# Taking the sixteen best scores straight from PSUM, beside the query projections

## The chip, the cores and the metric

The kernel runs on one core of a Trainium2 chip. The metric is the device time of one launch in microseconds (us). One launch computes one layer of the network over 1,024 tokens, all in fp32.

## The reference

The layer is an attention and state-space mixer followed by PEER, a feed-forward block that looks up single-neuron experts, and by a gated embedding. The change concerns only the look-up. Cut to that part, the reference is:

```python
q  = (u @ w_query).reshape(b, s, 8, 2, 128)            # 8 heads, 2 sides
sc = einsum("bshtd,htkd->bshtk", q, sub_keys)           # 128 scores a side
top_s, top_i = top_k(sc, 16)                            # sixteen best of each side
cand_s = top_s[..., 0, :, None] + top_s[..., 1, None, :]   # 256 sums
best_s, best_pos = top_k(cand_s, 16)
best_i = cand_i at best_pos                             # cand_i = top_i[0] * 128 + top_i[1]
gates  = softmax(best_s)
act    = gelu(einsum("td,ted->te", x, expert_u[best_i])) * gates
out    = einsum("te,ted->td", act, expert_v[best_i])
```

So each token picks 8 x 16 = 128 experts, and each of them needs one row of `expert_u` and one of `expert_v`, 4 KB each.

## The kernel before, in words

The tokens are cut into 8 tiles of 128 (one token per partition), and the tiles into 4 groups of 2. All five engines walk through one list of steps, `whole_program`, in the same order, and each does its own part of a step. A semaphore counts what others have finished.

**Ahead of the slots.** `before_slots` (L240) lists what must be done before the first expert is fetched: the whole front (mixer) of group 0, its query unit 0, the score selection for the first two (tile, head) pairs, and query unit 1, which stands ahead of these selections.

**The slots.** A slot n (`slot_steps`, L193) stands for one expert of every token of a tile: 128 slots a tile, 16 slots a head, 1,024 in all and 44 more at the end. In a slot POOL issues the indirect DMA (512 KB) that gathers 128 rows of `peer_u` (L868, a ring of 6) and, 44 slots later, 128 rows of `peer_v` (L880, a ring of 8). POOL takes both in turn. DVE multiplies a `peer_u` row with the normalised token and sums it (`dot`, L1575), and PE adds up the weighted `peer_v` rows (L2017). A gather of `peer_u` waits until DVE has done the dot product six slots earlier.

**Work beside the slots.** `beside_slots` (L248) hangs other steps on slots: query units 2 and 3 of group 0 on slots 2 to 20; the fronts of groups 1, 2 and 3 with their four query units on slots 22 to 204, 204 to 456 and 456 to 708 (`FRONT_SPANS`), where each step is placed by its share of the sum of the costs in `PACE`; and the gate of each tile later. Weight blocks of 1 MB come through a ring of 4 (L637); SP issues them in list order.

**A query unit** (`query_steps`, L169) is four head sides for two tiles: the projection (`p`, PE L1754, copied by ACT L956), the transposition (`q_t`, PE L1968, ACT L1121), and the score product (`q_s`, PE L1976), which fills one PSUM bank with 4 x 128 scores per token. ACT copies the bank to SBUF (L1128), SP writes it to HBM (`keep_scores`, L728, 256 KB), and later reads it back head by head (`scores_in`, L734, 128 KB). There are 32 such (tile, unit) pairs and 64 (tile, head) pairs kk.

**The selection** (`top`, L1519) for head kk goes over DVE in six steps, on slots 2, 4, 6, 8, 10 and 12 of the sixteen of an earlier head: steps 0 and 1 take the sixteen best of each side with `sixteen_best` (L1512: MAX8, FIND_INDEX8, MATCH_REPLACE8, MAX8, FIND_INDEX8), step 2 forms the 256 sums, step 3 takes the sixteen best of these, steps 4 and 5 work out the expert numbers. The read-back for the next head is issued on slot 8 (`s_in`).

PSUM banks are shared: `plan_banks` (L322) gives each step the bank that has lain unused longest, out of four once slot 25 is reached, and PE waits until the bank's last content has been taken.

## Time and profile before

| | |
|---|---|
| time before, median of 3 runs | 3769.55 us (3768.69 to 3770.98) |
| the profiled execution, its own time | 3753.05 us |
| its span in the trace | 3751.3 us |
| DVE busy | 2232.2 us (60%) |
| PE busy | 2475.1 us (66%) |
| POOL busy | 1964.5 us (52%) |
| moved by DMA | 1320.09 MB, mean 352 GB/s |

The page's header and its section 2 cut the span into 40 slices of 94 us: "DMA" is the mean busy share of the 16 DMA engines, in tenths. The windows give the same for chosen stretches. Their columns are: stretch and length; busy us of PE, of PE's weight loads, of DVE, ACT and POOL, each with its number of instructions in brackets; TensorE's granted clock; DMA share; GB/s. A window of one line has only the busy time of that line, and then the last three. DVE runs two instructions for a dot product at L1575, so half of that number is the slots passed. "Idle before" in a group of instructions is the time its engine stood still just ahead of them, and the arrow names what ended it. In a timeline the number in square brackets is that idle time for one instruction. A DMA share of slightly over 1 comes about because packets of two queues overlap on one DMA engine.

### The profile page before, as it was taken

The page shows a single profiled execution, that of the slowest core. Times are in us where ns is not written, and L with a number is a line of the kernel's source. Part 1 is how long each engine was busy: PE and PEld are TensorE (multiplying, and loading weights), DVE is VectorE, ACT ScalarE, POOL GpSimd, SP SyncE. Part 2 cuts the span into 40 slices and gives each one's busy share as a digit, 9 for nine tenths or more (in the row PEclk, how much of TensorE's full clock was granted, in tenths as well). Part 3 has the DMA queues.
Part 4 walks back from the last instruction along what each step waited for, and adds up shares of the span by engine and source line. Part 5 has one row for each costly group of instructions (what it writes and reads, how often), then busy time and mean ns, then how long its engine had stood idle before and what let it go on. Part 6 is the DMA issues. An engine that isn't in the chain of part 4 may idle for free. (4 is left out here: it accounts for less than half of the span.)

```text
span 3751.3 us, 33795 instructions
## 1 busy us (share of the span) xinstructions
PE 2475.1 (66%) x10840; PEld 1198.8 (32%) x10840; DVE 2232.2 (60%) x5446; ACT 765.6 (20%) x1750; POOL 1964.5 (52%) x2064
## 2 busy tenths in 40 slices
PE   8869688777777758666777767677725534443554
PEld 5644345443333434322333434322301101110111
DVE  2330868566556766675556766776556666666640
ACT  2331222231112222321122222311111111011010
POOL 0000455545555656555555656655656666666663
PEclk9879899778888777778888877778867666766778
DMA  7325899989999999999999999999999999999995
GB/s 229 114 74 188 317 398 385 352 315 355 406 405 404 376 346 390 384 350 406 405 405 403 369 364 384 382 377 407 401 376 381 372 387 382 378 385 377 367 377 202
DMA packets 427462, 1320.09 MB, mean 352 GB/s; under 512 B 54280, under 2 KB 75920, under 8 KB 425112
## 3 DMA queue, kind: packets, MB, share of 16 engines
q0 software_dynamic: 294912, 1073.87, 74.1%
q1 hardware_dynamic: 132376, 244.06, 17.9%
q8 instruction: 89, 1.46, 0.2%
q14 instruction: 85, 0.70, 0.0%
HBM read 1290.69 MB, written 32.60 MB: 353 GB/s over the span
## 5 line engine op out<-in xcount | busy, mean ns | idle before, releaser
L1575 DVE CUSTOM_DVE_ANT_0 u_ring<-u_ring,ps 128x1024 f32<-128x1024 f32 x1024 | 1231.7, 1217 | 551.4 <-DMA u_ring<-peer_u,idx_u 454.5
L868 POOL DMA_INDIRECT u_ring<-peer_u,idx_u x1024 | 981.5, 958 | 960.6 <-DVE idx_u L1553 379.8
L880 POOL DMA_INDIRECT v_ring<-peer_v,idx_v x1024 | 978.4, 955 | 787.1 <-PE ps L2017 340.4
L2017 PE MATMUL ps<-v_ring,spread 128*32 128x512 f32 x4096 | 752.7, 864 | 851.3 <-DMA v_ring<-peer_v,idx_v 744.2
L2017 PEld LDWEIGHTS ps<-v_ring,spread 128*32 128x32 f32 x4096 | 150.8, 138 | 1233.1 <-issue 1231.0
L1754 PE MATMUL ps<-front 128*128 128x512 f32 x1024 | 458.5, 604 | 2.1 <-ACT front L1117 2.1
L1754 PEld LDWEIGHTS ps<-front 128*128 128x128 f32 x1024 | 194.7, 194 | 271.5 <-issue 271.1
L1950 PE MATMUL ps<-front 128*128 128x512 f32 x512 | 232.8, 613 | 13.6 <-DVE front L1491 8.4
L1873 PE MATMUL ps<-front 128*128 128x256 f32 x768 | 197.8, 415 | 1.4 <-issue 1.4
L1873 PEld LDWEIGHTS ps<-front 128*128 128x128 f32 x768 | 156.1, 209 | 58.1 <-issue 34.6
L1950 PEld LDWEIGHTS ps<-front 128*128 128x128 f32 x512 | 98.9, 197 | 151.6 <-issue 151.6
L1382 DVE CUSTOM_DVE_ANT_0 front<-ps,front 128x640 f32<-128x640 f32 (+2 forms) x64 | 42.1, 658 | 154.2 <-PE ps L1841 59.0
L2047 PE MATMUL ps<-front 128*128 128x512 f32 x256 | 123.7, 637 | 13.9 <-issue 10.6
L1404 DVE SCALAR_TENSOR_TENSOR front<-front,taps 128x256 f32<-128x256 f32 x144 | 69.8, 485 | 100.0 <-ACT hist L1026 59.4
L1938 PE MATMUL ps<-front 128*128 128x512 f32 x256 | 120.8, 627 | 1.9 <-issue 1.9
L1841 PE MATMUL ps<-front 64*128 64x128 f32 x480 | 83.9, 328 | 31.9 <-DVE front L1375 9.8
L1851 PE MATMUL ps<-ident,front 128*128 128x128 f32 x240 | 49.0, 334 | 78.5 <-ACT front L1010 68.9
L1865 PE MATMUL ps<-front 128*128 128x64 f32 x480 | 76.7, 305 | 19.0 <-issue 18.6
L1841 PEld LDWEIGHTS ps<-front 64*128 64x128 f32 x480 | 72.1, 228 | 51.4 <-issue 40.0
L1149 ACT ACTIVATE dots<-dots 128x32 f32<-128x32 f32 x32 | 7.3, 229 | 396.9 <-DVE dots L1575 282.9
L1575 DVE DVE_READ_ACCUMULATOR2_ANT dots<- 128x1 f32 x1024 | 84.5, 83 | 0.0
L1865 PEld LDWEIGHTS ps<-front 128*128 128x128 f32 x480 | 70.2, 220 | 39.3 <-issue 36.4
(232 smaller groups left out, 2725.9 us busy)
## 6 DMA issues: line engine op xcount, KB each, us to landing
front<-w_in SPq DMA_DIRECT2D x76, 1024.0 KB
front<-w_out SPq DMA_DIRECT2D x32, 1024.0 KB
front<-peer_w_query SPq DMA_DIRECT2D x32, 1024.0 KB
u_ring<-peer_u,idx_u POOLq DMA_INDIRECT x1024
v_ring<-peer_v,idx_v POOLq DMA_INDIRECT x1024
front<-c_bias_all SPq DMA_DIRECT2D x32, 320.0 KB
front<-x SPq DMA_DIRECT2D x16, 512.0 KB
front<-cs_rows SPq DMA_DIRECT2D x8, 1024.0 KB
```

The source lines that it names most:

```text
L868: nc.gpsimd.indirect_dma_start(k.u_ring[:, n % RU, :], None, io["peer_u"][0], bass.IndirectOffsetOnAxis(ap=k.idx_u[:, t % 2, j:j + 1], axi ...
L880: nc.gpsimd.indirect_dma_start(row, None, io["peer_v"][0], bass.IndirectOffsetOnAxis(ap=k.idx_v[:, m % 2, column:column + 1], axis=0)).the ...
L1404: ins = stt(a, k.raw[:, c % 2, j:j + NG], k.taps[:, c, j:j + 1], a, ALU.mult, ALU.add)
L1575: nc.vector.tensor_tensor_reduce(out=row, in0=row, in1=k.un_ps, scale=1.0, scalar=0.0, op0=ALU.mult, op1=ALU.add, accum_out=k.dots[:, t % ...
L1754: last = mm(ps, k.uT[:, half * WCH + c, cols(t)], w[:, c, :], start=(half == 0 and c == 0), stop=(half == 1 and c == WCH - 1))
L1841: last = mm(ps[:, n * P:(n + 1) * P], k.qT_c[side, i // 2, cols(t)], k.kT_c[side, i // 2, kt % 6, :], start=True, stop=True)
L1865: last = mm(ps[:, at:at + HD], k.pT[:, no % 2, j, :], k.v_c[:, kt % 6, i * HD:(i + 1) * HD], start=(kt == c_keys(t)[0]), stop=(kt == t))
L1873: last = mm(ps[:, 0:NG], w[j // WCH][:, j % WCH, c % 4 * P:(c % 4 + 1) * P], k.uT[:, j, :], start=(j == 0), stop=(j == DCH - 1))
L1938: last = mm(ps, k.uT[:, c, cols(t)], w[c // WCH][:, c % WCH, :], start=(c == 0), stop=(c == DCH - 1))
L1950: last = mm(ps, k.yT[:, k.o_chunks[part] + j, cols(t)], w[:, j, :], start=(part == 0 and j == 0), stop=(part == 3 and j == WCH - 1))
L2017: last = mm(k.acc_ps[32 * j:32 * j + 32, half * 512:(half + 1) * 512], centres[:, at:at + 32], row[:, half * 512:(half + 1) * 512], start= ...
L2047: last = mm(ps[:, half * 512:(half + 1) * 512], k.fT[:, c, :], k.wg[:, c, half * 512:(half + 1) * 512], start=(c == 0), stop=(c == DCH - 1))
```

## The change

The sixteen best of each side are taken by DVE directly from the PSUM bank, in new steps `q_top` (one for each side of a unit, four for each tile and unit, 128 in all). Their values and key numbers (converted to float) lie in `best_out` and go to HBM, 64 KB a (tile, unit) pair; they are read back two heads at a time. ACT's copy of the scores goes. `top` keeps four steps, on slots 2, 4, 6 and 8. `spread_tops` puts two `q_top` steps behind each of the following steps of the query unit. `PACE` counts each `q_top` as 1.6, so the query units take a larger part of each front's slots. Query unit 1 of group 0 now stands behind the selections of the first two heads.

```diff
-        out += [(st, t, u) for st in ("q_t", "q_s") for t in tiles_of(g)]
+        out += [(st, t, u) for t in tiles_of(g) for st in ("q_t", "q_s")]
+    return spread_tops(out)
+
+def spread_tops(steps):
+    out, late = [], []
+    for step in steps + [None, None]:
+        if step:
+            out.append(step)
+        now, late = late[:2], late[2:]
+        out += now
+        if step and step[0] == "q_s":
+            late += [("q_top", *step[1:], i) for i in range(4)]
...
-            n2_t=1.2, q_t=1.2, q_s=1.2)
+            n2_t=1.2, q_t=1.2, q_s=1.2, q_top=1.6)
...
-    if 2 <= k < TILES * PH and 2 <= s <= 12 and s % 2 == 0:
+    if 2 <= k < TILES * PH and 2 <= s <= 8 and s % 2 == 0:
         out.append(("top", k, s // 2 - 1))
...
-    if k + 1 < TILES * PH and s == 8:
-        out.append(("s_in", k + 1))
+    if k % 2 and k + 1 < TILES * PH and s == 10:
+        out.append(("s_in", (k + 1) // 2))
...
-    out = front_steps(0) + query_steps(0, [0]) + [("un_in", 0), ("s_in", 0), ("s_in", 1), ("un", 0)] + query_steps(0, [1])
+    out = front_steps(0) + query_steps(0, [0]) + [("un_in", 0), ("s_in", 0), ("un", 0)]
     for k in range(2):
-        out += [("top", k, i) for i in range(6)] + [("g_exp", k), ("g_norm", k)]
-    return out + [("s_in", 2)]
+        out += [("top", k, i) for i in range(4)] + [("g_exp", k), ("g_norm", k)]
+    return out + query_steps(0, [1]) + [("s_in", 1)]
...
     def keep_scores(t, u):
-        copied(("q_s", t, u))
         n = score_no(t, u)
+        sp.wait_ge(k.best_kept, 4 * (n + 1))
...
-    def scores_in(kk):
-        n = score_no(kk // PH, kk % PH // 2)
+    def scores_in(pair):
+        n = score_no(pair // QUERY_UNITS, pair % QUERY_UNITS)
         sp.wait_ge(k.sc_out[n % 2], (n // 2 + 1) * 16)
-        if kk >= 2:
-            sp.wait_ge(k.idx_full, kk - 1)
+        if pair >= 2:
+            sp.wait_ge(k.idx_full, 2 * (pair - 1))
...
-    def q_s(t, u):
-        _, ps, copied_ = filled(("q_s", t, u))
-        o = t // GT * QUERY_UNITS + u
-        if o:
-            act.wait_ge(k.sc_out[t % GT], o * 16)
-        act_fn(k.sc[:, t % GT, :], ps, ACT.Copy).then_inc(copied_, 1)
...
+    def q_top(t, u, i):
+        _, ps, copied_ = filled(("q_s", t, u))
+        o, place = t // GT * QUERY_UNITS + u, t % GT
+        if o and i == 0:
+            dve.wait_ge(k.sc_out[place], o * 16)
+        src, vals = ps[:, i * PK:(i + 1) * PK], k.best_out[:, place, 0, i, :]
+        chain.link(nc.vector.max(vals[:, 0:8], src))
+        chain.link(nc.vector.max_index(k.keys_out[:, 0:8], vals[:, 0:8], src))
+        nc.vector.match_replace(k.beaten, vals[:, 0:8], src, -3e38).then_inc(copied_, 1)
+        dve.wait_ge(copied_, k.bank["q_s", t, u].begin + i + 1)
+        chain.link(nc.vector.max(vals[:, 8:16], k.beaten))
+        chain.link(nc.vector.max_index(k.keys_out[:, 8:16], vals[:, 8:16], k.beaten))
+        nc.vector.tensor_copy(k.best_out[:, place, 1, i, :], k.keys_out).then_inc(k.best_kept, 1)
+        n = t // GT * GT * QUERY_UNITS + u * GT + place
+        dve.wait_ge(k.best_kept, 4 * n + i + 1)
```

In `top` the two `sixteen_best` calls over 128 scores and the conversion of the key numbers are gone; the sums, the sixteen best of them and the arithmetic of expert numbers stay, and read `s_in` instead of `top` and `top_f`.

## Rows read from the trace of the kernel before

**Rows 1.** The page: busy tenths of the DMA engines in 40 slices.

```profile
DMA  7325899989999999999999999999999999999995
```

**Rows 2.** Windows by stage: ahead of the slots, slots 0 to 48, fronts of groups 1 to 3, the rest.

```profile
0.00:385.00 385.00, 317.40 (x1136) 197.06 (x1137) 105.29 (x276) 114.33 (x273) 4.67 (x16) 0.88 0.46 150
...
400.00:498.00 98.00, 54.53 (x197) 31.34 (x200) 89.85 (x222) 22.05 (x44) 52.01 (x54) 0.81 0.95 351
498.00:1070.00 572.00, 451.01 (x2026) 237.81 (x2019) 364.15 (x906) 148.62 (x347) 301.12 (x314) 0.85 0.97 370
1070.00:1905.00 835.00, 590.74 (x2733) 292.72 (x2732) 539.53 (x1324) 184.52 (x425) 483.23 (x504) 0.81 0.99 385
1905.00:2720.00 815.00, 577.75 (x2668) 289.83 (x2666) 539.89 (x1324) 180.91 (x420) 480.37 (x502) 0.81 1.00 387
2720.00:3640.00 920.00, 413.30 (x1786) 124.72 (x1786) 574.44 (x1344) 101.38 (x216) 597.97 (x628) 0.68 0.98 379
```

**Rows 3.** The waits in total, longest first, and DVE's for a row of values.

```profile
DVE u_ring L1575 <- DMA u_ring<-peer_u,idx_u: 454.5, 277, 6.0
...
DVE idx_v L1567 <- remote: 55.6, 12, 13.4
```

**Rows 4.** Timeline of DVE, the selection for head 0 ahead of the slots (side 0 of two).

```profile
375.29 0.30 DVE L1513 MAX8 top<-s_in 128x8 f32<-128x128 f32 x1 [26.30 <-DMA s_in<-scores]
...
377.14 0.30 DVE L1513 MAX8 top<-s_in 128x8 f32<-128x128 f32 x1
...
378.98 0.18 DVE L1526 CAST top_f<-top_i 128x32 f32<-128x32 uint32 x1
379.20 0.42 DVE L1527 TENSOR_TENSOR cand<-top 128x256 f32<-128x256 f32 x1
```

**Rows 5.** Timeline of ACT, SP, DVE and POOL, from the first scores to the first dot product.

```profile
368.69 0.60 ACT L1128 ACTIVATE front<-ps 128x512 f32<-128x512 f32 x1 [0.39 <-PE ps L1976]
...
369.31 1.26 SPq L731 DMA_DIRECT2D scores<-front  x2
...
372.17 0.81 SPq L739 DMA_DIRECT2D s_in<-scores  x2
...
385.65 1.09 POOL L868 DMA_INDIRECT u_ring<-peer_u,idx_u  x1 [379.82 <-DVE idx_u L1553]
...
399.68 1.19 ACT L956 ACTIVATE front<-ps 128x512 f32<-128x512 f32 x2
400.15 1.22 DVE L1575 CUSTOM_DVE_ANT_0 u_ring<-u_ring,ps 128x1024 f32<-128x1024 f32 x1
...
402.85 0.60 ACT L1128 ACTIVATE front<-ps 128x512 f32<-128x512 f32 x1 [0.63 <-PE ps L1976]
```

**Rows 6.** Groups by shape on DVE: the same operation with a source in PSUM and in SBUF.

```profile
L1471 DVE TENSOR_TENSOR front<-ps,front 128x512 f32<-128x512 f32 x16 | 11.0, 687 | 5.9 <-PE ps L1925 3.7 <-remote 2.2
...
L1464 DVE TENSOR_TENSOR front<-front 128x512 f32<-128x512 f32 x16 | 11.0, 685 | 0.0
```

**Rows 7.** The page: DMA queues and their share of 16 engines.

```profile
q0 software_dynamic: 294912, 1073.87, 74.1%
q1 hardware_dynamic: 132376, 244.06, 17.9%
```

**Rows 8.** The DMA issues by tensor: KB of one.

```profile
scores<-front SPq DMA_DIRECT2D x32, 256.0 KB
s_in<-scores SPq DMA_DIRECT2D x64, 128.0 KB
```

**Rows 9.** Windows: slots 178 to 204, the query stage of group 1.

```profile
973.00:1067.00 94.00, 78.51 (x310) 35.27 (x309) 49.73 (x126) 18.18 (x37) 52.78 (x56) 0.93 1.03 406
```

**Rows 10.** Windows of L1575 alone: slots 0 to 44, and the stretch above.

```profile
400.00:492.00 92.00, 52.37 (x89) 0.81 0.95 347
...
973.00:1067.00 94.00, 31.57 (x53) 0.93 1.03 406
```

**Rows 11.** DMA queue of SP: what its issue waited for, the wait that goes.

```profile
SPq L738 <- DVE idx_u L1553: 203.3, 8, 51.1
```

More of the change, by code:

```diff
@@ L325, in plan_banks @@
     singles = dict(n1_t=1, sub=1, a_k=GT, a_turn=1, c_turn=1, a_t=1, c_u=1, x=3, z=1, dt=1, cs=5, b_turn=2, b_cb=2, b_off=1, b_diag=1,
-                   b_state=1, y_t=1, n2_t=1, q_t=1, q_s=1, rows=1, w_turn=1, g_p=1, g_t=1)
+                   b_state=1, y_t=1, n2_t=1, q_t=1, q_s=4, rows=1, w_turn=1, g_p=1, g_t=1)
     early = before_slots()
@@ L453, in __init__ @@
         self.q = in_yT(0, 1024).rearrange("p (b n) -> p b n", n=UNIT)
-        self.sc = in_yT(1024, 1024).rearrange("p (b n) -> p b n", n=UNIT)
+        self.best_out = in_yT(1024, 256).rearrange("p (b k s n) -> p b k s n", b=GT, k=2, n=TOPK)
+        self.keys_out = self.front.bitcast(U32)[:, 10240 + 1280:10240 + 1280 + TOPK]
+        self.beaten = in_yT(1280 + TOPK, PK)
         self.xn = arena(6144, 2048).rearrange("p (t n) -> p t n", n=D)
@@ L503, in __init__ @@
         self.wT = sb("wT", [P, PART])
[L504 to L507 removed]
+        self.s_in = sb("s_in", [P, 2, 2, 4, TOPK])
         self.cand = sb("cand", [P, TOPK, TOPK])
@@ L530, in __init__ @@
         self.after = dram("after", (SEQ, D))
-        self.scores = dram("scores", (TILES * PH, P, 2 * PK))
+        self.scores = dram("scores", (TILES * QUERY_UNITS, P, 8 * TOPK))
         self.cs_rows = dram("cs_rows", (TILES * B_HEADS, P))
@@ L815, in sync_program @@
             keep_tiles(*at)
-        elif kind == "q_s":
-            keep_scores(*at)
+        elif kind == "q_top" and at[2] == 3:
+            keep_scores(*at[:2])
         elif kind == "s_in":
@@ L1242, in scalar_program @@
             q_t(*at)
-        elif kind == "q_s":
-            q_s(*at)
         elif kind == "g_exp":
@@ L1517, in sixteen_best @@
         chain.link(nc.vector.max_index(idx[:, 8:16], vals[:, 8:16], scratch))
-    def top(kk, step):
-        if step < 2:
-            if step == 0:
-                dve.wait_ge(k.sc_here[kk % 2], (kk // 2 + 1) * 16)
-            part = k.s_in[:, kk % 2, step * PK:(step + 1) * PK]
-            sixteen_best(k.top[:, step, :], k.top_i[:, step, :], part, part)
-        elif step == 2:
-            chain.link(nc.vector.tensor_copy(k.top_f[:], k.top_i[:]))
-            chain.link(tt(k.cand[:], k.top[:, 0, :].unsqueeze(2).broadcast_to([P, TOPK, TOPK]),
-                          k.top[:, 1:2, :].broadcast_to([P, TOPK, TOPK]), ALU.add))
-        elif step == 3:
+    def q_top(t, u, i):
[13 more added lines that the diff above has]
+        dve.wait_ge(k.best_kept, 4 * n + i + 1)
+    def top(kk, step):
+        kept = k.s_in[:, kk // 2 % 2]
+        sides = slice(kk % 2 * 2, kk % 2 * 2 + 2)
+        if step == 0:
+            if kk % 2 == 0:
+                dve.wait_ge(k.sc_here[kk // 2 % 2], (kk // 4 + 1) * 16)
+            first, second = kept[:, 0, kk % 2 * 2, :], kept[:, 0, kk % 2 * 2 + 1, :]
+            chain.link(tt(k.cand[:], first.unsqueeze(2).broadcast_to([P, TOPK, TOPK]),
+                          second.unsqueeze(1).broadcast_to([P, TOPK, TOPK]), ALU.add))
+        elif step == 1:
             if kk:
@@ L1533, in top @@
             sixteen_best(k.best[:], k.best_i[:], flat, flat)
-        elif step == 4:
+        elif step == 2:
             if kk == 0:
@@ L1542, in top @@
             by_side = k.hot[:].rearrange("p (a s) b -> p a s b", a=2)
-            chain.link(tt(by_side, by_side, k.top_f[:].unsqueeze(2).broadcast_to([P, 2, TOPK, TOPK]), ALU.mult))
+            chain.link(tt(by_side, by_side, kept[:, 1, sides, :].unsqueeze(2).broadcast_to([P, 2, TOPK, TOPK]), ALU.mult))
             chain.link(nc.vector.tensor_reduce(k.halves[:], by_side, axis=AX.X, op=ALU.add))
@@ L1662, in vector_program @@
             n2(*at)
+        elif kind == "q_top":
+            q_top(*at)
         elif kind == "top":
```

14 lines of the change are left out of this document (5 added, 9 removed).

## The prediction

> **What bounds the kernel now.** I read the busy shares of the 40 slices first, then windows by stage, the waits, and last the timeline around the first gather. The slices show DMA at 9 tenths or full in nearly every slice from the sixth on, and at 2 to 7 before [rows 1]. The windows put it in numbers. Ahead of the first gather (0 to 385 us) the share is 0.46: PE's front sets the time there. From 498 to 3640 us it is 0.97, 0.99, 1.00 and 0.98, while DVE is at 60 to 67% and POOL at 50 to 65% [rows 2]. DVE's longest wait is for a gathered `peer_u` row, 454.5 us in all [rows 3]. So from slot 48 on the DMA engines are the limit, and an engine counts only where it makes them run dry. Full they read 1.03 and 406 GB/s, as in a query stage [rows 9]; measured against 1.03, the four stages lose 33, 32, 24 and 45 us, 134 us together. Between 400 and 498 us both are near their limit: DVE 89.85 of 98 us busy, DMA 0.95 [rows 2]. Here DVE sets the pace of the slots, because `peer_v` is not yet gathered. Two currencies follow: a microsecond of DVE on the way to slot 44 is paid in full, one taken out later is paid only in as far as DMA ran dry for it; a byte saved is worth its DMA time after slot 44.
>
> **Price of one new step.** `sixteen_best` over 128 scores runs from 375.29 to 377.14, 1.85 us; the conversion of the indices with its gap takes 0.22 us [rows 4]. `q_top` is the same chain with a conversion of its own: 2.07 us. Its source is now PSUM. No MAX8 on PSUM is in the trace; an addition of 128x512 takes 687 ns with a source in PSUM and 685 ns from SBUF [rows 6], so I take no surcharge (bounds: 0, and 5% of the 1.85 us, some 3 us over all that lie ahead of slot 44). 128 steps cost 265 us of DVE, against the 64 x 3.9 = 250 us that go (375.29 to 379.20, two sides and the conversion): DVE's sum is nearly unchanged, its place is not. ACT loses 32 copies of 0.60 us [rows 5], which nobody waited long for: 0.
>
> **A. To the first gather and the first dot product.** Before, ACT's copy starts at 368.69, the write is issued at 369.31, the read at 372.17, DVE begins at 375.29, and POOL gathers at 385.65 [rows 4, 5]. After, DVE takes four sides of tile 0 first: 368.7 + 4 x 2.07 = 377.0. Its write can go, but SP stands in list order before the write of tile 1, whose four sides DVE ends at 385.3; only then can it issue the read. With 1.1 us of issuing and the 3.1 us from issue to data (372.17 to 375.29) DVE has the sixteens at 389.5. What is left of the selection took 379.20 to 385.65, 6.4 us: first gather at 395.9, **+10.2 us**. The first dot product stood at 400.15, 14.5 us after the first gather; 3.9 us of that are side selections that go: 406.5. But now query unit 1 stands between. PE's projection of it needs nobody and has 40 us for it, but ACT copies it only after `g_exp(1)`, at about 406.1; from that copy to filled scores the same chain took 399.68 to 402.85 in unit 2, 3.2 us, or 2.9 to the first tile [rows 5]. Then eight `q_top`, 16.6 us, follow on DVE, and the dot product behind them: 406.1 + 2.9 + 16.6 = 425.6. **Together +25.5 us.** What waits behind: the dot products free the ring of six, so POOL stands still after six gathers, and the DMA queues have little else: the weight ring of four fills and waits for PE. Bounds 17 (part of the eight steps overlapping the chain) and 30.
>
> **B. Slots 0 to 44.** 44.5 dot products took 92 us [rows 10]. Units 2 and 3 put 16 `q_top` on slots 3 to 19: +33.1 us. Three selections in this stretch lose 3.9 us each: -11.7. Net +21.4. DVE stood still about 8 us of the 98, mostly for gathers [rows 2]; with DMA now idle I let half of it vanish: **+18 us**. Bounds 13 and 24. Nothing on DMA can be done ahead to make this good, since the front of group 1 hangs on slots 22 and later.
>
> **C. Bytes.** Scores go out as 32 x 256 KB and come back as 64 x 128 KB [rows 8], 16.8 MB; after, 32 x 64 KB each way, 4.2 MB. The hardware queue took 17.9% of the span for 244.06 MB [rows 7], 2.75 us a MB, so 12.6 MB are 34.6 us of DMA time. 2 MB of it fall ahead of slot 44, and full engines read 1.03: **-28 us**. The packets halve to 512 B. If one costs what a packet of 1 KB does, only their number counts, which halves too: -14 us. Bounds -34 and -14. The Trainium skill speaks against the size of this saving: "DMA: Bandwidth & Descriptors", section "Measured", gives 0.95 us for a 64 KB transfer and says that transfers below 64 KB are dominated by descriptors. An estimate by that page alone, 64 transfers of 0.95 us, is 61 us, which is more than the 46 us of the bytes before at the trace's price, so by it the saving is gone and the sum of this prediction rises to some +50 us. The trace has one side of it only: other transfers fill the engines while a small one waits (share 0.97 to 1.00), so I keep the price by bytes.
>
> **D. Query stages of groups 1 to 3.** 32 `q_top` a group, 66 us of DVE, now fall into the query units. `PACE` makes room: a unit counts 27 instead of 14.2, so the queries take 108 of 395 in place of 57 of 344: about 45 slots of group 1 (159 to 204), 64 of groups 2 and 3. A slot moves 1.05 MB (1073.87 MB over 1,024 slots [rows 7]), the eight weight blocks 8.4 MB. Group 1: 56 MB at 406 GB/s are 138 us of DMA. DVE: 45 dot products of 1.18 us [rows 10], 53; 2.8 selections of 6.6 us, 18; 66; 5 for the rest: 142 us. DVE is thus at the limit, in a stage where it was 53% busy [rows 9], and it now waits itself for `q_s`, which ACT did before. What is queued behind that wait: dot products, hence POOL, hence both rings. Eight such waits of up to 2.9 us would be 23 us; I take DVE's surplus and a little under half of the waits, **+13 us**. Groups 2 and 3: 187 us of DMA against 174 of DVE, so waits fit in between: **0**, up to 23 each. PE also finds a bank held longer; part of the same bound.
>
> **E. What DVE's relief gives back.** Outside the query stages each head costs DVE 3.9 us less. Some of the 134 us of dry engines comes from that; but one clear part does not, DVE's waits for a row of values at L1567, 55.6 us [rows 3], and the two longest pieces of a selection, steps 3 and 4, stay and now stand on slots 4 and 6. The same front work is also squeezed into fewer slots (136 for 156), against the relief. **-6 us**, bounds 0 and -25. SP's wait for `idx_u`, 203.3 us in all [rows 11], vanishes as well; weights are a ring of four ahead, so I give it nothing, bound -5.
>
> **Sum.** +25.5 + 18 - 28 + 13 - 6 = +22.5 us. The profiled execution took 3753.05 us itself, 3751.3 of it span, and lies 16.5 us below the median of 3769.55; so its successor's profile should read about 3775, and the median **3792 us**.
>
> **Rivals.** (1) *It gets faster, because the side selections are what dries the DMA engines.* If relief returns half of the 134 us, 67 us, the sum is 28.5 - 67 = -38: 3731 us. The point from which it decides is 29 us, 22% of the dry time. For it: they are DVE work of 3.9 us a head that holds back dot products, hence the ring. Against it: DVE is only 62 to 67% busy, and L1567 and the front's own chains stay. (2) *DVE and PE go in lockstep in all query stages.* Each of the 24 (tile, unit) pairs then costs its 2.9 us, 70 us, less the 13 already counted, and with half of the surplus of groups 2 and 3 absorbed some +35 more: 3827 us. For it: one engine now does what two did, and four banks are shared. Against it: groups 2 and 3 have slack by the sum above. (3) *It comes out even.* The first-order loss A+B, 43.5 us, shrinks to its lower bound 30, DVE is not short in group 1 (0), and C and E give 30: 3770 us. For it: the share from 400 to 498 us is already 0.95 [rows 2], so part of DVE's time there hides behind DMA. (4) *Small packets keep their price*, C = -14: 3806 us. It lies inside the first case's range.
>
> **How the numbers follow.** Forecast with (4) inside it 0.52, its own range 3778 to 3808; (2) 0.18; (3) 0.13; (1) 0.17. A change of 0.2%, 7.5 us, is about what this measurement can tell from none. Faster: (1) and a little of (3), 0.18. Same: the rest of (3) and the lower edge of the forecast, 0.13. Slower: 0.69. The range takes in (3) and most of (2): 3754 to 3830.
>
> **What the profile after would show.** First POOL gather near 396, first dot product near 425, slot 44 near 535 us instead of 492, with a DMA share well under 0.95 in between: A and B right. MAX8 with source PSUM at 290 to 300 ns: the price right. Hardware queue near 231 MB and 17% of the span: C. DVE over 85% busy around slots 159 to 204 with idle time at MAX8 ended by PE L1976: D. The prediction is wrong if the later stages run shorter by more than 40 us together (rival 1), or if the first dot product starts before 415.

## The result, and the profile after

| | before | changed |
|---|---|---|
| median of 4 runs each | 3770.14 us (3768.69 to 3770.98) | 3835.28 us (3826.84 to 3841.59) |
| ratio, with 95% interval | | 1.0166 [1.0143, 1.0188] |
| profiled execution, its own time | 3753.05 us | 3826.84 us |
| span in the trace | 3751.3 us | 3825.1 us |

The change makes the kernel slower by 65 us. The forecast had the sign, was 43 us too low, and the time lies 5 us above the upper edge of its range. From the page of the changed kernel, the same lines as in [rows 1, 7] and the busy tenths of DVE:

```profile
span 3825.1 us, 33780 instructions
...
DVE  2331876556696656665775756857765555555530
...
DMA  7314689888999999999999989999999999999995
...
q0 software_dynamic: 294912, 1073.87, 73.3%
q1 hardware_dynamic: 123672, 231.48, 16.7%
```

Against [rows 1] the DMA line has 4 and 6 where 5 and 8 stood in the fourth and fifth slice, and eights in the sixth, eighth and tenth slice where nines stood. The hardware queue moves 12.6 MB less, as intended: 244.06 MB [rows 7] became 231.48.

**Where the time went, by slots.** The surest ruler is the dot product: one per slot, two instructions each. These are windows of that line alone, cut at slots 44, 80, 96, 204, 708 and 1023; the columns are stretch, length, DVE's busy time (instructions), PE's granted clock, DMA share and GB/s. The changed kernel:

```profile
423.40:538.40 115.00, 52.47 (x87) 0.75 0.78 267
538.40:672.70 134.30, 43.39 (x74) 0.90 0.95 363
672.70:746.10 73.40, 19.14 (x32) 0.79 0.84 313
746.10:1148.40 402.30, 130.28 (x216) 0.82 0.95 364
1148.40:2809.20 1660.80, 605.90 (x1008) 0.81 0.99 379
2809.20:3712.50 903.30, 384.03 (x630) 0.68 0.99 379
```

The kernel before, same slots:

```profile
400.10:491.90 91.80, 52.29 (x88) 0.81 0.95 347
491.90:611.10 119.20, 43.64 (x72) 0.91 1.02 394
611.10:658.70 47.60, 19.15 (x31) 0.89 1.00 385
658.70:1067.50 408.80, 130.70 (x218) 0.82 0.95 361
1067.50:2727.80 1660.30, 608.05 (x1008) 0.81 1.00 386
2727.80:3640.70 912.90, 383.14 (x630) 0.68 0.99 379
```

Subtracted row by row: the first dot product is 23.3 us late; slots 0 to 44 lose 23.2; slots 44 to 80 lose 15.1; slots 80 to 96 lose 25.8; slots 96 to 204 give back 6.5; 204 to 708 are even (+0.5); 708 to 1023 give back 9.6; behind the last dot product 2.0 are lost. That is 73.8 us, the difference of the spans. (The profiled execution of before lies 17.1 us below its median, that of the changed kernel 8.4, so some 9 of the 73.8 are the choice of execution. A second pair of traces, changed_again and before_again below, has +28, +23, +10 and +25 us up to slot 96, and gives back 25 behind it instead of 14.) Two things are to be seen: all of the net loss lies ahead of slot 96, and almost half of it, 41 us between slots 44 and 96, lies where the forecast had put nothing.

**The start**, from the timelines of DVE, SP, POOL and ACT of the changed kernel (a number in square brackets is the idle time just before):

```profile
367.70 0.30 DVE L1531 MAX8 front<-ps 128x8 f32<-128x128 f32 x1 [19.51 <-PE ps L1999]
...
376.18 8.60 SPq L744 DMA_DIRECT2D scores<-front  x2
...
385.30 0.43 SPq L753 DMA_DIRECT2D s_in<-scores  x1
...
388.81 0.43 DVE L1548 TENSOR_TENSOR cand<-s_in 128x256 f32<-128x256 f32 x1 [4.39 <-DMA s_in<-scores]
...
395.25 1.09 POOL L882 DMA_INDIRECT u_ring<-peer_u,idx_u  x1 [389.44 <-DVE idx_u L1574]
...
402.37 1.06 ACT L970 ACTIVATE front<-ps 128x512 f32<-128x512 f32 x2
...
406.92 0.30 DVE L1531 MAX8 front<-ps 128x8 f32<-128x128 f32 x1 [3.98 <-PE ps L1999]
...
423.45 1.22 DVE L1596 CUSTOM_DVE_ANT_0 u_ring<-u_ring,ps 128x1024 f32<-128x1024 f32 x1
...
424.95 0.93 POOL L882 DMA_INDIRECT u_ring<-peer_u,idx_u  x1 [22.05 <-DVE dots L1596]
```

SP issues the write of tile 0 at 376.18; the row holds both writes (x2), and its 8.60 us reach to the end of the second, which could go only once DVE was through with the four sides of tile 1. The read-back can only follow. POOL issues six gathers and then stands still for 22.05 us until the first dot product frees a place of the ring.

**The new steps.** The groups of DVE by shape (busy us, mean ns, idle time before and its releasers), and below them the first MAX8 of a side in the kernel before, whose source lay in SBUF:

```profile
L1531 DVE MAX8 front<-ps 128x8 f32<-128x128 f32 x128 | 37.9, 296 | 39.0 <-PE ps L1999 34.7 <-remote 2.0 <-DVE cand L1548 0.6
...
L1535 DVE MAX8 front<-front 128x8 f32<-128x128 f32 x128 | 37.8, 295 | 6.8 <-DVE front L1533 2.5
...
L1537 DVE CAST front<-front 128x16 f32<-128x16 uint32 x128 | 24.0, 188 | 8.9 <-remote 3.5 <-DVE front L1536 1.0
```

```profile
L1513 DVE MAX8 top<-s_in 128x8 f32<-128x128 f32 x128 | 37.1, 290 | 26.4 <-DMA s_in<-scores 26.3
```

Of the 34.7 us that DVE waited for scores, 23.5 are the two waits at the start shown above; the other 30 pairs share 11 us.

**The query stage.** The windows of all engines (PE, PE's weight loads, DVE, ACT, POOL; then clock, DMA share, GB/s). Slots 154 to 204 of the changed kernel:

```profile
974.00:1148.00 174.00, 110.06 (x472) 47.46 (x464) 140.11 (x456) 29.18 (x58) 95.40 (x100) 0.81 1.03 402
```

The same slots of the kernel before:

```profile
887.00:1067.00 180.00, 151.24 (x534) 64.33 (x533) 96.57 (x228) 26.28 (x54) 94.20 (x99) 0.91 1.03 403
```

DVE went from 54 to 81% busy, and the stage got no longer: DMA is full in both. But the two don't hold the same steps: the first transposition of a query unit stands on slot 161 after the change, on 181 before. The run that has the steps of the changed kernel there without `q_top` is the squeeze by itself (squeeze_again, set 3):

```profile
940.80:1106.80 166.00, 106.98 (x452) 46.18 (x448) 94.38 (x226) 29.04 (x59) 93.26 (x97) 0.81 1.03 406
```

Against these 166.0 us the changed kernel's 174.0 are 8 us more (172.6, 7 more, in changed_again).

**The stretch that nobody had priced.** DVE's waits in slots 80 to 96 of the changed kernel (us in all, times, longest):

```profile
DVE front L1387 <- PE ps L1864: 18.2, 4, 10.0
DVE front L1387 <- DMA front<-c_bias_all: 14.2, 1, 14.2
```

Before, the same slots had no such wait; its longest was one of 3.5 us for ACT. That is in part because this work lay elsewhere then. L1387 is `c_s`, DVE's part of the banded attention C of group 1's front, which adds a bias to PE's scores. PE, DVE and ACT take turns there, DVE stands in the listed order with its dot products, and the front has 136 slots for what had 156, so this attention begins at slot 89 in place of 98. Slots 80 to 112 hold its start in both kernels: they took 129.6 us against 108.0, so 22 us are lost and not only moved, and DVE's wait for the scores there (us in all, times, longest) grew from the first of these lines, before, to the second, changed:

```profile
DVE front L1382 <- PE ps L1841: 6.8, 2, 5.8
```

```profile
DVE front L1387 <- PE ps L1864: 31.1, 7, 10.0
```

The bias came late because SP issues in list order too, behind weight blocks that wait for a place in the ring:

```profile
641.75 57.54 SPq L650 DMA_DIRECT2D front<-w_in  x6
699.39 1.72 SPq L659 DMA_DIRECT2D front<-c_bias_all  x2
```

Two suspects for the 41 us between slots 44 and 96, then: the late load, and too few slots. The experiments had to tell them apart.

### The profile page after: what moved, and what is told of

It reads as the page before. It is cut to its first block and busy times, and to the rows that moved or that the text cites. A ratio compares the mean times of both kernels' runs of the same rounds, so it can differ in the third digit from the quotient of the medians.

```text
span 3825.1 us, 33780 instructions
## 1 busy us (share of the span) xinstructions
PE 2477.0 (65%) x10840; PEld 1208.6 (32%) x10840; DVE 2250.1 (59%) x5510; ACT 751.5 (20%) x1721; POOL 1953.1 (51%) x2064
## 3 DMA queue, kind: packets, MB, share of 16 engines
q1 hardware_dynamic: 123672, 231.48, 16.7%
## 5 line engine op out<-in xcount | busy, mean ns | idle before, releaser
L882 POOL DMA_INDIRECT u_ring<-peer_u,idx_u x1024 | 971.1, 948 | 1066.9 <-DVE dots L1596 406.2
L2040 PE MATMUL ps<-v_ring,spread 128*32 128x512 f32 x4096 | 741.7, 859 | 868.7 <-DMA v_ring<-peer_v,idx_v 760.6
L1777 PEld LDWEIGHTS ps<-front 128*128 128x128 f32 x1024 | 195.3, 195 | 272.8 <-issue 272.5
L1896 PE MATMUL ps<-front 128*128 128x256 f32 x768 | 189.8, 402 | 3.2 <-ACT hist L1040 1.6
L1896 PEld LDWEIGHTS ps<-front 128*128 128x128 f32 x768 | 151.1, 202 | 43.8 <-issue 22.0
L1387 DVE CUSTOM_DVE_ANT_0 front<-ps,front 128x640 f32<-128x640 f32 (+2 forms) x64 | 42.1, 657 | 205.5 <-PE ps L1864 94.8
L1973 PEld LDWEIGHTS ps<-front 128*128 128x128 f32 x512 | 97.9, 194 | 139.2 <-issue 139.1
L1331 DVE TENSOR_REDUCE hm<-front 128x8 f32<-128x512 f32 (+1 forms) x32 | 18.6, 585 | 109.8 <-ACT front L947 82.8
L970 ACT ACTIVATE front<-ps 128x512 f32<-128x512 f32 x32 | 19.0, 596 | 325.2 <-PE ps L1777 222.8
```

The source lines that it names most:

```text
L882: nc.gpsimd.indirect_dma_start(k.u_ring[:, n % RU, :], None, io["peer_u"][0], bass.IndirectOffsetOnAxis(ap=k.idx_u[:, t % 2, j:j + 1], axi ...
L1777: last = mm(ps, k.uT[:, half * WCH + c, cols(t)], w[:, c, :], start=(half == 0 and c == 0), stop=(half == 1 and c == WCH - 1))
L1896: last = mm(ps[:, 0:NG], w[j // WCH][:, j % WCH, c % 4 * P:(c % 4 + 1) * P], k.uT[:, j, :], start=(j == 0), stop=(j == DCH - 1))
L1973: last = mm(ps, k.yT[:, k.o_chunks[part] + j, cols(t)], w[:, j, :], start=(part == 0 and j == 0), stop=(part == 3 and j == WCH - 1))
L2040: last = mm(k.acc_ps[32 * j:32 * j + 32, half * 512:(half + 1) * 512], centres[:, at:at + 32], row[:, half * 512:(half + 1) * 512], start= ...
```

## The experiments

"before" was timed beside each set on the same chip: 3659.81 us (set 1), 3777.72 (set 2), 3779.22 (set 3), 3659.99 (set 4) and 3656.97 (set 5). Ratios are against it. Each set ran on one chip, sets 4 and 5 on the same one and sets 1, 2 and 3 each on another, so a difference between sets also holds a difference between chips. The text says "late by" for the start of a slot's dot product against that of `before_again`, a trace of set 3. The first dot product alone lay between 394.5 and 401.2 us in traces whose start is that of the kernel before, so a few us of any such lateness are scatter. Of the longer edits the first or the telling lines are shown.

### Set 1: the parts of the change

**squeeze_alone**: the kernel before, whose front is pressed into as few slots as in the changed one, nothing else.

```diff
-            n2_t=1.2, q_t=1.2, q_s=1.2)
+            n2_t=1.2, q_t=1.2, q_s=7.6)
```

> The kernel before, with one figure of PACE changed: q_s counts 7.6 instead of 1.2, so that the query units take the same 108 of 395 parts of a front's slots as after the change and the mixer steps are pressed into the slots ahead of them; no other edit. Theory 1 (the changed kernel loses some 25 to 30 us in the front of group 1 because its mixer steps come in fewer slots, so that slots wait for a chain of PE, ACT, DVE and late loads): slower than before by 15 to 30 us, 3785 to 3800, with slots 64 to 154 late and some of it given back in slots 159 to 204. Theory 2 (the squeeze is harmless because the same bytes and the same work fall into the same 182 slots; the loss comes from the new steps themselves): within 6 us of 3770.

Measured 3687.67 us, 1.0080 [1.0064, 1.0097]: +28 us (23 to 35) with not one instruction more. Slots 80 to 96 take 77.9 us, where the changed kernel took 73.4. The squeeze is a cost of its own, not a detail of the relief.

**pace_zero**: the changed kernel with the new steps counted as nothing, so that the front keeps the slots that it had.

```diff
-            n2_t=1.2, q_t=1.2, q_s=1.2, q_top=1.6)
+            n2_t=1.2, q_t=1.2, q_s=1.2, q_top=0.0)
```

> The changed kernel with q_top counting 0 in PACE instead of 1.6: the steps are the same, the mixer has its old slots again, and 32 q_top a group fall into some 26 to 37 slots. Theory 1 (squeeze): it gets back 15 to 30 us of the 65, 3805 to 3820, unless the crowded query stage takes it again. Theory 2 (what counts is DVE's crowding in the query stages): slower than the changed kernel by 10 us or more, 3845 or above, because DVE has some 66 us of new steps in 94 us.

Measured 3707.26 us, 1.0140 [1.0118, 1.0163]. Slots 80 to 96 take 48.6 us again, but slots 178 to 204, the query stage, come out 28 us later than they went in. The loss is not avoided, it changes its place; the 15 to 30 us that the first theory wanted back can't be seen (1.0140 here, 1.0146 and 1.0166 for the changed kernel on other chips).

**quarter_bytes**: the kernel before, where only 64 of the 256 scores per token and head go out and back. It saves the bytes of the change, 12.6 MB, at an unchanged number of packets, and adds no work but one POOL instruction at the start. It leaves out three quarters of the keys. The edit of the read-back; the write is narrowed in the same way:

```diff
-        sp.dma_start(k.s_in[:, kk % 2, :], k.scores[kk]).then_inc(k.sc_here[kk % 2], 16)
+        sp.dma_start(k.s_in[:, kk % 2, 96:160], k.scores[kk][:, 96:160]).then_inc(k.sc_here[kk % 2], 16)
```

> The kernel before, but only 64 of each 256 scores (32 of either side) go out to HBM and come back; the other scores that DVE searches are constants far below, set once. It leaves out three quarters of the keys. The packets keep their number, 16384, and have 256 B instead of 1 KB; DVE's work is the same. By bytes (2.75 us a MB, 12.6 MB): 28 us faster than before, 3742. If a small packet costs what a larger one does, or if the score transfers are hidden anyway: no change, 3765 to 3772. In between, the price is mixed.

Measured 3636.28 us, 0.9939 [0.9921, 0.9957]: -23.5 us. Its queue, from the page:

```profile
q1 hardware_dynamic: 132376, 231.48, 17.6%
```

The same 132,376 packets as before [rows 7], and the time fell by most of what the bytes are worth at the price of term C. The queue's own time says the same of the changed kernel: 16.7% of 3825.1 us there and 17.6% of 3634.0 us here are 639 and 640 us for the same 231.48 MB, with 8,704 packets fewer in the changed kernel. The section "Measured" of "DMA: Bandwidth & Descriptors" in the Trainium skill has transfers below 64 KB dominated by descriptors. That section's table is of loads issued from GpSimd, these are transfers that SP issues; and read-backs of 32 KB that kept their number of packets gave most of the bytes' worth all the same, beside engines that are full. Here the measurement decides.

**group0_old**: the changed kernel, but group 0 (start and slots 0 to 44) as before.

```diff
+    if g == 0:
+        for u in units:
+            out += project(g, f"q{u}")
+            out += [(st, t, u) for st in ("q_t", "q_s") for t in tiles_of(g)]
+        return out
```

> The changed kernel, but group 0 (tiles 0 and 1, whose units 0 to 3 stand ahead of slot 20) goes the old way: ACT copies the scores, they go through HBM, and the side selections stand on slots 2 and 4 of their heads; groups 1 to 3 go the new way with the new pace. Theory 1 (the 47 us by which slot 44 is late are carried to the end whole): slot 44 near 492 us as before the change, and the end 45 us or more earlier than the changed kernel, 3785 to 3792. Theory 2 (the start is caught up later by the DMA engines, and the loss is the later stages'): less than 25 us earlier, 3810 or more. What then remains above 3770 is the later stages' own cost less the bytes.

Measured 3664.11 us, 1.0019 [1.0008, 1.0030]. Slot 44 is late by 2 us, not 51, and slot 96 by 33. Without the start's loss the change is nearly even on this chip.

### Set 2: is the late load of the bias the squeeze's cost?

**changed_again**: the changed kernel once more, for this chip.

> The changed kernel itself, once more, beside the other runs of this call, so that differences between them are taken on one chip. The ratio to the kernel before should be 1.015 to 1.019 as measured the first time. Theory 1 (the start's loss and the squeezed front of group 1 add up) says further that the old way for group 0 alone, which measured 1.002, stands 45 to 60 us below it.

Measured 3839.26 us, 1.0146 [1.0123, 1.0170].

**squeeze_bias_early**: squeeze_alone, with the first two bias loads of groups 1 to 3 issued ahead of attention A. The edit of the list; SP's wait is changed too, as shown under before_bias_early.

```diff
+    early = [("c_bias", g, 0), ("c_bias", g, 1)]
-    out += projected_steps(g) + blend(a_steps(g), x_steps(g)) + [("x_silu", g), ("c_bias", g, 0), ("c_bias", g, 1)]
+    out += projected_steps(g) + (early if g else []) + blend(a_steps(g), x_steps(g)) + [("x_silu", g)] + ([] if g else early)
```

> The kernel before with q_s counting 7.6 (measured 28 us slower than before), and with one more edit: SP issues the first two loads of attention C's bias for groups 1 to 3 ahead of the steps of mixer A and of the x projection (as soon as the x tiles, whose place they take, have been read), not behind the last weight blocks of the x projection. Theory 1a (of the 30 us lost between slots 88 and 96 about half is DVE's wait of 14.6 us for this late load, behind which the dot products stand): 10 to 18 us faster than the squeeze alone, and the wait at L1382 for the bias gone. Theory 1b (the chain of PE and DVE through the scores of attention C sets the pace there, and the load is only the last to come): less than 6 us, the wait moves to PE L1841.

Measured 3779.53 us, 1.0002 [0.9983, 1.0020]. It looked like proof: the squeeze's loss is gone. But the windows of the dot product in slots 80 to 96 did not agree:

```profile
622.90:691.30 68.40, 19.13 (x32) 0.78 0.84 311
```

68.4 us, where 47.6 stood before and 73.4 in the changed kernel. The total was right and the place wrong; set 4 cleared it up.

**group0_old_bias_early**: group0_old with the same edit.

> Group 0 the old way, groups 1 to 3 the new way with the new pace (measured 4 us slower than before), and the bias of attention C loaded early as in the run above. Theory 1a: 10 to 18 us less, that is 6 to 14 us faster than the kernel before. Theory 1b: within 6 us of group 0 the old way alone.

Measured 3776.01 us, 0.9987 [0.9974, 1.0000]: a gain of 2 us where 6 to 14 had been expected.

**group0_old_pace_zero**: group 0 as before, groups 1 to 3 changed, and no squeeze.

> Group 0 the old way, groups 1 to 3 the new way, and q_top counting 0 in PACE, so that the mixer keeps its old slots. If the squeeze costs its 28 us here as it did alone and the bytes give their 20: 24 us less than group 0 the old way with the new pace, some 20 us faster than the kernel before. If the crowded query stages cost (in the changed kernel with q_top at 0, slots 178 to 204 lost 29 us, part of it given back): only 5 to 12 us less, 0 to 8 us faster than before.

Measured 3824.88 us, 1.0104 [1.0080, 1.0128]; I had expected a gain. Its windows for slots 178 to 204:

```profile
981.00:1109.40 128.40, 92.70 (x359) 42.44 (x357) 108.73 (x415) 21.20 (x41) 56.18 (x59) 0.86 0.91 348
```

And the same slots of the kernel before, profiled in set 3:

```profile
971.80:1067.80 96.00, 79.03 (x305) 35.32 (x306) 49.94 (x127) 17.44 (x37) 52.44 (x55) 0.93 1.03 407
```

DVE is 85% busy, DMA falls from 1.03 to 0.91, and 26 slots take 32.4 us more. The query stages of groups 2 and 3 do the same (slots 419 to 456: 152.2 us for 120.0; 671 to 708: 142.3 for 123.8). So the room that `PACE` makes is needed, and it is paid for by the front.

### Set 3: the two losses, each by itself

**before_again**: the kernel before, for a profile of this chip.

> The kernel before itself, for a trace that belongs to the same chip as the three runs beside it (the chips of the first two calls gave 3660 and 3778 us for this same kernel, so that the slots' times of one chip can't be held against those of the other). Ratio 1.000 within its interval.

Measured 3776.71 us, 0.9997 [0.9983, 1.0011].

**squeeze_again**: squeeze_alone once more.

> The kernel before with q_s counting 7.6, once more, on the chip of its reference trace. Theory 1 (a stall of 25 to 30 us between slots 88 and 96 of group 1's front, of which little is given back): 1.005 to 1.010. If the stall is given back where the DMA engines are slower, as the run with the early bias load leaves possible: within 0.3% of 1, and the slots after 204 show no lag. Both on slots 80 to 96: a lag that jumps by 25 us or more.

Measured 3820.45 us, 1.0116 [1.0089, 1.0143]: +41 us (34 to 54). Late by 10 us at slot 44, 23 at 80, 49 at 96, 39 at 204, 33 at slot 1023. The windows of the dot product for slots 44 to 80 and 80 to 96:

```profile
498.20:633.40 135.20, 43.46 (x74) 0.87 0.94 360
633.40:707.20 73.80, 19.14 (x32) 0.79 0.81 300
```

These are the changed kernel's 134.3 and 73.4 us to within a microsecond.

**group0_new_alone**: group 0 the new way, groups 1 to 3 with the old steps and the old pace; the counterpart of group0_old. Its edit is shown against group0_old:

```diff
-    if g == 0:
+    if g:
         for u in units:
             out += project(g, f"q{u}")
             out += [(st, t, u) for st in ("q_t", "q_s") for t in tiles_of(g)]
         return out
```

> The reverse of group 0 the old way: group 0 goes the new way (q_top ahead of the slots and on slots 3 to 19, unit 1 behind the first selections), groups 1 to 3 go the old way with the old pace. Theory 1 (the start's loss is carried whole): slot 44 late by 46 to 48 us and the end by 40 to 48 us, ratio 1.011 to 1.013. Theory 2 (DMA catches up later): less than 25 us, ratio under 1.007.

Measured 3831.87 us, 1.0139 [1.0099, 1.0179]: +53 us (37 to 68), with group 0's quarter of the saved bytes in it. Windows of the dot product, slots 0 to 44, 44 to 80 and 80 to 96:

```profile
421.90:535.10 113.20, 52.56 (x88) 0.73 0.77 269
535.10:663.80 128.70, 43.54 (x72) 0.88 1.00 385
663.80:713.60 49.80, 19.05 (x31) 0.90 0.92 347
```

Late by 26 us at slot 0, 47 at slot 44, then between 54 and 62 to the end (56 at slot 1023). What the start loses is not made up here, and slots 80 to 96 are ordinary.

**group0_old_again**: group0_old on this chip.

> Group 0 the old way, groups 1 to 3 the new way with the new pace, beside the squeeze alone on one chip. Both have the same pace; it differs from the squeeze alone by the new steps in the query stages of groups 1 to 3 and by 9.4 MB less over the DMA queues. If the bytes count as in the run with a quarter of them (24 us for 12.6 MB, so 18 us) and the new steps cost nothing in stages of 45 to 64 slots: 18 us below the squeeze. If DVE's new waits and work cost: level with it or above it.

Measured 3812.63 us, 1.0099 [1.0071, 1.0127]; in set 1 it was 1.0019. The intervals don't meet. Late by 5 us at slot 44, 42 at 96, 48 at 204, 26 at slot 1023.

### Set 4: the early load without the squeeze, and a way between

**changed_bias_early**: the changed kernel with the early load.

> The changed kernel with the one edit of the early bias load (groups 1 to 3), nothing else. Theory 1 (the changed kernel's loss is the start plus the squeezed fronts, and the late bias load is what the squeeze costs most): 25 to 40 us less than the changed kernel, ratio 1.005 to 1.010, which leaves the start's loss of some 47 us less the bytes. Theory 2 (the squeeze overlaps with the start's loss, so that in the changed kernel little of it is left to win): less than 12 us, ratio above 1.012.

Measured 3668.52 us, 1.0031 [1.0020, 1.0042].

**before_bias_early**: the kernel before with it, the control that set 2 lacked.

```diff
-            filled(("a_s", g * GT + GT - 1, A_PAIRS - 1))
+            if g:
+                sp.wait_ge(k.xn_full, (g + 1) * GT)
+            else:
+                filled(("a_s", g * GT + GT - 1, A_PAIRS - 1))
```

> The kernel before with the early bias load alone. Its trace shows DVE's wait for the bias with 24.8 us in all, 5.3 of it in group 1. Theory 1: there the load is mostly in time, so no more than 10 us faster, ratio 0.997 to 1.001. If the ratio is 0.99 or less, the regain of the runs with the squeeze was this edit's own worth and not the squeeze's.

Measured 3628.04 us, 0.9924 [0.9905, 0.9943]: -32 us, the fastest of all. I had expected at most 10. So most of what the load regained in set 2 can be its worth without the squeeze. With it in both, the change costs 1.1% (1.0031 against 0.9924, one chip), and the squeeze alone 0.8% (1.0002 against 0.9924), if the gain of the load on this chip holds for that of set 2. The late load as the squeeze's main cost, my first theory, has lost its ground. The slots show more. With the load early in both, slots 80 to 112 take 119.5 us in the changed kernel and 96.0 in this one, on the same chip, so 24 us are lost there with no late load. DVE's wait for PE's scores in these slots, of changed_bias_early and then of this kernel:

```profile
DVE front L1391 <- PE ps L1868: 41.0, 9, 10.5
```

```profile
DVE front L1386 <- PE ps L1845: 7.7, 2, 4.9
```

Every kernel with the full squeeze has 30 to 41 us of this wait in slots 80 to 112, with the load early or late (only squeeze_roomy_c below, where attention C has its slots back, has 19), and those with none have 3 to 13. It comes with the squeeze and not with the late load. SP's timelines, first of this kernel, then of the kernel before:

```profile
547.73 0.94 SPq L647 DMA_DIRECT2D front<-c_bias_all  x2
...
672.49 10.29 SPq L647 DMA_DIRECT2D front<-c_bias_all  x2
```

```profile
672.19 19.67 SPq L646 DMA_DIRECT2D front<-c_bias_all  x4
```

The windows of 640 to 760 us, again this kernel first:

```profile
640.00:760.00 120.00, 98.94 (x509) 58.45 (x508) 81.02 (x218) 34.09 (x80) 67.50 (x71) 0.82 1.00 387
```

```profile
640.00:760.00 120.00, 89.92 (x417) 52.88 (x418) 71.57 (x193) 30.80 (x69) 58.40 (x62) 0.76 0.93 353
```

The first two loads of the bias are issued 124 us earlier, and DMA runs at 387 GB/s where it ran at 353 on the chip of set 3. DVE's waits for the bias over the whole span, of this kernel:

```profile
DVE front L1386 <- DMA front<-c_bias_all: 6.8, 2, 4.8
```

And of before_again:

```profile
DVE front L1382 <- DMA front<-c_bias_all: 25.3, 5, 10.0
```

The trace of the kernel before has 34.8 us of them, so 18 to 28 us of waiting vanish for the 32 us gained. With the squeeze these waits were longer, 48.6 us in squeeze_alone and 42.1 in squeeze_again, and 8.2 in squeeze_bias_early: the late load may have a share in the squeeze's loss, some 7 to 23 us of waiting.

**group0_old_half_bias** and **group0_old_half**: group 0 as before, `q_top` counted 0.8 for half of the squeeze, with the early load and without.

```diff
-            n2_t=1.2, q_t=1.2, q_s=1.2, q_top=1.6)
+            n2_t=1.2, q_t=1.2, q_s=1.2, q_top=0.8)
```

> Group 0 the old way, q_top counting 0.8 instead of 1.6, bias early: between the full pace (squeezed fronts, measured 0.9987 with the bias early) and pace zero (query stages short by some 33 us each in groups 1 and 2, 1.0104). If both costs are convex in the pace, this is the best version: 8 to 20 us faster than before, 0.995 to 0.998. If they add up straight: 1.004.

> The same with the bias load in its old place. It tells how much of the squeeze is left at half the pace: if the late bias load still stalls DVE by 10 us or more between slots 88 and 104, 10 to 20 us above the run beside it; if half the squeeze is harmless, within 6 us of it.

Measured 3643.17 us, 0.9962 [0.9950, 0.9974], and 3674.31 us, 1.0047 [1.0030, 1.0063]. The way between lies between the two readings of group0_old with the whole room, 1.0019 and 1.0099, and the better one of the two stays 0.4% behind before_bias_early, which has nothing of the change. On this one chip the load can be judged fairly: the half-squeezed kernel costs 14 us over its control with the load late (3674.31 against 3659.99) and 15 with it early (3643.17 against 3628.04). No part of the late load is to be seen in that loss.

### Set 5: attention C, or the whole front?

**squeeze_roomy_c**: squeeze_alone, but attention C counted 1.3 times, so that it has the slots of the kernel before; the rest of the front gives them up.

```diff
-            c_s=1.2, c_u=1.2, c_v=0.9,
+            c_s=1.56, c_u=1.56, c_v=1.17,
```

> The kernel before with the squeezed front (q_s counted as 7.6), but the steps of attention C are counted 1.3 times, so that they hold as many slots as in the kernel before (group 1: 32 slots, group 2: 51, where the squeeze alone gives 30 and 50); all the rest of the front gives up the room. Theory chain (the squeeze costs because PE and DVE take turns in attention C and have too few slots for it): most of the loss of 0.8 to 1.2% goes, ratio 1.000 to 1.004, and the slots in which C starts (80 to 96) no longer stand out. Rival whole front (any front work in fewer slots costs the same): ratio 1.008 to 1.012, with the loss only moved to neighbouring slots.

Measured 3685.61 us, 1.0081 [1.0066, 1.0096]. The windows of the dot product, slots 80 to 96 and 96 to 112:

```profile
622.00:691.40 69.40, 19.32 (x34) 0.80 0.88 330
691.40:738.30 46.90, 19.09 (x31) 0.78 1.01 390
```

In squeeze_alone, on another chip, these took 77.9 and 57.5 us. So group 1 gains 19 us there, and yet the time is that of squeeze_alone, 1.0081 against 1.0080: what C gets back is lost elsewhere, 8 us of it between slots 204 and 708.

**before_tight_c**: the kernel before with attention C counted 0.8 times: C has the slots that the squeeze gives it, the rest has more.

```diff
-            c_s=1.2, c_u=1.2, c_v=0.9,
+            c_s=0.96, c_u=0.96, c_v=0.72,
```

> The kernel before with no squeeze, but the steps of attention C counted 0.8 times, so that they get the slots that the squeeze gives them (group 1: 30, group 2: 50) and the rest of the front gets what they give up. Theory chain: a good part of the squeeze's loss appears, ratio 1.004 to 1.010. Rival whole front: no loss, 0.998 to 1.002.

Measured 3669.65 us, 1.0036 [1.0022, 1.0049]: +13 us, between the two expectations. Attention C is where a shortage of slots shows first, and pressing it alone costs something; relieving it alone gains nothing. The rival, the whole front, has the better of it, though its "no loss" for this run did not come true either.

## Why the prediction was right, and where it failed

**What bounds the kernel** held: from slot 96 on the DMA share is 0.95 to 0.99, and quarter_bytes gained.

**The price of a step** held. Eight steps took from 406.92 to the dot product at 423.45, 16.5 us against 16.6. The source in PSUM has a small surcharge, inside the bounds: MAX8 took 296 ns where the same pass from SBUF took 290, FIND_INDEX8 290 for 285 and MATCH_REPLACE8 281 for 276, 2 us over all 128 steps.

**A, the start, was right.** Predicted: first gather at 395.9, first dot product at 425.6. Measured: 395.25 and 423.45. DVE started query unit 1 at 406.92, not 409.0, and that is all of the difference. Two smaller misses partly cancel in it, which is luck: ACT began the copy at 402.37 and not at 406.1, and from there to the filled scores it took 4.6 us and not 2.9.

**B was right, a little low.** Predicted +18 for slots 0 to 44, bounds 13 and 24; measured +23.2. Part of that is the squeeze, which begins at slot 22: without it (group0_new_alone) these slots lose 21.5 us, the 21.4 that stood there with none of DVE's idle time used up. A and B together: 43.5 predicted, 46.5 measured in this trace, and group0_new_alone shows them unshrunk at the end (+53 us by the clock, 37 to 68). Rival (3), which let them shrink to 30, is refuted.

**C was right.** Predicted -28; quarter_bytes gave -23.5 (by its interval -16 to -29). With the packets unchanged in number, rival (4) would have had nothing left of it. What the prediction worked out from the Trainium skill's page, that the saving would vanish, did not come true either.

**D is not refuted.** Predicted +13 for the query stage of group 1. Against the kernel before, slots 154 to 204 took 174 us for 180, but before the change these slots hold front steps that now stand ahead of them. Against the squeeze alone, which has the same steps there without `q_top`, it is 174.0 and 172.6 us for 166.0 and 166.1: +7 to +8. The signs for it failed in part: DVE reached 81%, not over 85%, and waited 3.6 us at MAX8 in the whole stage. The sum of bytes behind it, 56 MB for 45 slots, was too low too: squeeze_alone moved 63 MB in them, 154.1 us at 407 GB/s. Rival (2) fell in the changed kernel: the 30 pairs behind the start share 11 us of waiting for scores, not 70. Its 3827 us came nearest to the measured time, by luck and not by its mechanism. The pace is why: without it (group0_old_pace_zero) the three stages lose 32.4, 32.2 and 18.5 us.

**E is the step that failed.** It said "The same front work is also squeezed into fewer slots (136 for 156), against the relief" and let it rest in a sum of -6. The squeeze was seen and got no price, and the bounds, 0 and -25, left no room for a loss. By itself it costs +28 us (squeeze_alone) and +41 us (squeeze_again). The relief that was to stand against it can't be seen: from the squeeze's ratio and three quarters of the bytes' 0.6%, group0_old should stand at 1.0034 and 1.0070 with no relief at all, and stood at 1.0019 and 1.0099. The term was about +35, not -6: 41 us, against a miss of 43 in all. The other terms were off by about +9 (A and B), +5 (C) and -5 (D, against the squeeze); these lie within the uncertainty of the runs. Rival (1), half of the dry time back, is refuted with it.

**The account.** Start alone +53 (a quarter of the bytes is in it), squeeze alone +28 to +41, the other three quarters of the bytes -18: +63 to +76, against a measured +65 (first runs) and +61.5 (changed_again). These come from several chips and each has an uncertainty of some 6 to 15 us, so no further term is needed, and D's 7 to 8 us, or a relief of that size, can't be told apart in it.

**Why the squeeze costs**, as far as shown. The slots take more time while the same front work rides on fewer of them: DMA falls from 1.00 to 0.84 in slots 80 to 96, with DVE waiting in the turns of PE, DVE and ACT. In slots 80 to 112 DVE's wait for the scores of attention C is 30 to 41 us with the full squeeze, 15 to 16 with the half, and 3 to 13 with none; with the full squeeze and the old slots for attention C it is 19, and yet no time is won. Later slots give back only a part of it, 16 of 49 us in squeeze_again; that they can't give back more because DMA is full there already is argued from the shares of 0.99 to 1.03, not shown. The squeeze costs without the late bias too: with the load early in both, slots 80 to 112 lose 24 us in the changed kernel, and at half of the squeeze the loss is 14 us with the load late and 15 with it early. How large its share is at the full squeeze stays open, since no pair of runs has that on one chip. The slots of attention C alone are not the main part either (set 5). Which of the front's other chains takes the rest stays open.

**The best version** of those run is before_bias_early, 0.9924 [0.9905, 0.9943]: the kernel before with one load moved. Taking the sixteen best from PSUM added nothing to it in any form that was run.

## What to carry to other kernels

When a list of steps is spread over a fixed span by their costs, giving one step room takes it from all others: price this squeeze as a term of its own (here 28 to 41 us, more than the bytes that the change saved), by changing the cost alone in the old kernel. Work that is moved ahead of the point at which DMA becomes the bound was paid in full here, and no later slack returned it (group0_new_alone). And an edit that seems to cure a loss needs its control on the kernel without the loss: the early load seemed to take the changed kernel from between 1.0146 and 1.0166 down to 1.0031 (on another chip), and was worth 0.8% on its own.

## What the runs showed of the hardware

- The kernel before took 3657 to 3660 us in sets 1, 4 and 5 (two chips) and 3770 to 3779 us in the others, 3% apart, each set on one chip and steady within itself. The size of an effect moved too: group0_old read 1.0019 beside 3660 us and 1.0099 beside 3779 us, the squeeze 1.0080 and 1.0116. A loss below 1% is to be read beside its own control.
- Bytes counted even in small packets beside full DMA engines: 12.6 MB less at the same 132,376 packets, with packets of 256 B, were worth 23.5 us.
- MAX8 over 128x128 fp32 costs nearly the same with its source in PSUM and in SBUF: 296 ns against 290 for the same pass of the kernel before, and 295 for the second pass in both.
